# Three edits around the expert stage of a streaming-encoder block: skipped empty slots, a divided last load, one load issued earlier

## What is computed

```python
xf = x.reshape(B * T, D)                      # 512 x 1024
g_prob = softmax(xf @ rg_w + rg_b)            # 4 groups, the best one is taken
e_logits = ...                                # 8 experts in that group, top 2 taken, weights normalised
for g in range(N_GROUPS):                     # 4 groups x 8 experts = 32 experts
    hg = silu(xf @ w_gate[g]) * (xf @ w_up[g])        # 1024 -> 256
    y = y + (hg * combine[:, g]) @ w_down[g]          # 256 -> 1024
h = LayerNorm(alpha * h + y)
```

## Time and profile before

| | |
|---|---|
| median of 3 runs | 785.86 us (784.17 to 786.19) |
| the profiled execution | 784.38 us |
| its span | 782.6 us |
| granted TensorE clock, mean | 0.978 |
| TensorE matmul busy | 711.1 us, 91% |
| VectorE, ScalarE, GpSimd busy | 48%, 38%, 33% |
| DMA, mean over the span | 203 GB/s |
| weights of the experts | 96 MB in 96 loads of 1 MB |

### The profile page before, as it was taken

How to read it: one execution, slowest core, us unless ns; L and a number is a source line. 1 busy time by engine, 2 the same in 40 slices (tenths; PEclk the granted TensorE clock), 3 DMA queues, 4 the chain that set the end, 5 groups by cost and what they waited for, 6 DMA issues and landing times.

```text
span 782.6 us, 11844 instructions
## 1 busy us (share of the span) xinstructions
PE 711.1 (91%) x4296; PEld 501.9 (64%) x4296; DVE 377.2 (48%) x984; ACT 295.2 (38%) x604; POOL 259.9 (33%) x315
## 2 busy tenths in 40 slices
PE   7999999999999999999999999999999998887810
PEld 6865886777777777776888777655555554444400
DVE  2436998877577766648221346635211111111137
ACT  4345326667565555654320312123222222111111
POOL 3721541222234322137882000023333333233213
PEclk9999999999999999999999999999999999999965
DMA  8511231111123111016523690899999999999762
GB/s 229 160 54 55 60 102 54 55 55 54 55 61 102 55 55 54 30 33 226 173 80 108 233 384 28 304 397 417 416 417 419 418 417 419 417 417 418 326 226 121
DMA packets 57890, 158.57 MB, mean 203 GB/s; under 512 B 8558, under 2 KB 37238, under 8 KB 45552
## 3 DMA queue, kind: packets, MB, share of 16 engines
q1 hardware_dynamic: 52640, 149.15, 50.0%
q0 software_dynamic: 5200, 8.76, 3.1%
HBM read 153.60 MB, written 12.58 MB: 212 GB/s over the span
## 4 chain that ended last, share of the span: by engine, by line
PE 79%; DMA 9%; DVE 6%; SPq 2%; ACT 2%; issue 1%; POOL 0%; POOLq 0%; ACTq 0%; DVEq 0%
PE psum L849 36%; PE psum L1137 10%; DMA arena<-in_w_up_dram 7%; PE psum L1160 6%; PE psum L836 4%; PE psum L924 4%; PE psum L982 2%; PE psum L960 2%; PE psum L1056 2%; PE psum L830 2%; PE psum L976 2%; PE psum L782 1%; PE psum L894 1%; PE psum L1152 1%; DVE arena L1542 1%
## 5 line engine op out<-in xcount | busy, mean ns | idle before, releaser
L849 PE MATMUL psum<-arena,arena 128*128 128x512 f32 (+1 forms) x1296 | 316.9, 395 | 2.4 <-DVE arena L1542 1.3
L849 PEld LDWEIGHTS psum<-arena,arena 128*128 128x128 f32 x1296 | 235.1, 188 | 63.7 <-issue 15.4
L648 POOL TENSOR_TENSOR arena<-arena,arena 128x256 fp32r<-128x256 f32 (+1 forms) x139 | 145.1, 1079 | 237.5 <-ACT arena L1188 237.5
L1137 PE MATMUL psum<-arena,gate_a_T 128*64 128x256 f32 x1024 | 116.7, 380 | 11.5 <-DMA arena<-in_w_up_dram 11.4
L1137 PEld LDWEIGHTS psum<-arena,gate_a_T 128*64 128x64 f32 x1024 | 76.1, 137 | 60.7 <-issue 30.1
L1775 DVE COPY gate_a_T<-psum 128x128 f32<-128x128 f32 x32 | 9.4, 293 | 175.5 <-PE psum L1152 175.5
L1160 PE MATMUL psum<-arena,gate_a_T 128*64 128x512 f32 x256 | 62.0, 604 | 13.1 <-DVE gate_a_T L1775 13.1
L1188 ACT ACTIVATE arena<-arena 128x2048 fp32r<-128x2048 f32 x27 | 51.6, 1910 | 36.8 <-DMA arena<-in_w_branch_b_dram 26.7
L1278 ACT ACTIVATE arena<-arena,negm 128x193 f32<-128x193 f32 (+5 forms) x128 | 62.5, 493 | 3.6 <-DVE negm L1512 3.6
L1288 ACT ACTIVATE arena<-psum 128x1024 f32<-128x1024 f32 (+3 forms) x48 | 37.2, 775 | 69.5 <-PE psum L960 50.4
L728 POOL DMA_INDIRECT pair_rows<-gate_a_T,idx x32 | 33.2, 1038 | 62.3 <-ACT gate_a_T L1393 62.3
(11 more groups left out here) (233 smaller groups left out, 842.3 us busy)
## 6 DMA issues: line engine op xcount, KB each, us to landing
arena<-in_w_gate_dram SPq DMA_DIRECT2D x32, 1024.0 KB, 23.3
arena<-in_w_up_dram SPq DMA_DIRECT2D x32, 1024.0 KB, 27.2
arena<-in_w_down_dram SPq DMA_DIRECT2D x32, 1024.0 KB, 27.7
arena<-in_w_in_dram SPq DMA_DIRECT2D x19, 1024.0 KB, 5.3
arena<-in_w_branch_a_dram SPq DMA_DIRECT2D x4, 1024.0 KB, 5.2
arena<-in_w_branch_b_dram SPq DMA_DIRECT2D x4, 1024.0 KB, 5.3
arena<-in_w_out_dram SPq DMA_DIRECT2D x4, 1024.0 KB, 8.6
arena<-pair_rows SPq DMA_DIRECT2D x8, 512.0 KB, 7.3
```

The costliest lines, as they stand in the source:

```text
L648: nc.gpsimd.tensor_tensor(lo[:, k], raw[:, k], hi[:, k], ALU.subtract).then_inc(w_split, DT // n)
L849: ins = nc.tensor.matmul(ps[:, columns(kind)], wp[:, k, col:col + P], xp[:, k, columns(kind)], start=k == 0 and p == 0, stop=k == DT - 1 a ...
L1137: ins = nc.tensor.matmul(psum[CAP * g:CAP * g + CAP, 2 + s % 2, 0:FF], xgT[s % 2][:, k % 4, k // 4, :], ex_gu[slot][:, g, k, :], start=k = ...
```

## The change

Three edits that don't touch each other:

1. `tok_first` goes. The gathers of experts 2, 3 and 4 take their indices from `tok_i`, with the bounds check that the later gathers have, and wait for it.
2. Gate and up of expert 31 (slot 1, `LAST`) are loaded by four DMAs of 512 KB: k rows 0 to 3 of gate and of up, counted by a new semaphore `gu_front`, then k rows 4 to 7 of both. TensorE's `start(31)` waits for the front, and before k row 4 for the rest.
3. The load of down of expert 3 is issued right behind up of expert 4, ahead of the wait for `h1_ready` and the store of tile 3.

```diff
+LAST = (NE - 1) % EXS
...
-        tok_first = sb("tok_first", [P, XGS], I32)
...
+            def gate_up_part(e, slot, k0, k1, landed):
+                for g, w in enumerate((w_gate, w_up)):
+                    sp.dma_start(ex_gu[slot][:, g, k0:k1, :],
+                                 w[0, e].rearrange("(p k) f -> p k f", p=P)[:, k0:k1, :]).then_inc(landed, 16)
...
                     sp.wait_ge(unit_done, UNIT["out", 7] + 1)
                     up(4, 4)
+                    down(3, 3)
                 sp.wait_ge(h1_ready, t + 1)
                 sp.dma_start(h1_dram[2 * t * P:2 * (t + 1) * P, :].rearrange("(p h) c -> p (h c)", h=2), h1[:, t, :]
                              ).then_inc(h1_stored, 16)
-            down(3, 3)
             down(4, 4)
...
             for b in range((NE - EXS) // EXS * EXS, NE - EXS):
-                if b + 1 < NE - EXS:
+                if b + 2 < NE - EXS:
                     refill_gate_up(b + 1, b % EXS + 1)
+                elif b + 1 < NE - EXS:
+                    sp.wait_ge(gu_done, b + 2)
+                    gate_up_part(NE - 1, LAST, 0, DT // 2, gu_front)
+                    gate_up_part(NE - 1, LAST, DT // 2, DT, gu_landed[LAST])
                 refill_down(b, b % EXS)
...
                 pool.indirect_dma_start(out=xg[to], out_offset=None, in_=h1_dram,
-                                        in_offset=bass.IndirectOffsetOnAxis(ap=tok_first[:, n:n + 1], axis=0)
-                                        ).then_inc(xg_landed[to], 16)
-            pool.wait_ge(tok_ready, 2)
+                                        in_offset=bass.IndirectOffsetOnAxis(ap=tok_i[:, PEX + n:PEX + n + 1], axis=0),
+                                        bounds_check=2 * T - 1, oob_is_err=False).then_inc(xg_landed[to], 16)
...
-                pe.wait_ge(gu_landed[slot], use * 32 + 32)
+                if isinstance(b, int) and b == NE - 1:
+                    pe.wait_ge(gu_front, 32)
+                else:
+                    pe.wait_ge(gu_landed[slot], use * 32 + 32)
                 pe.wait_ge(xgt_copied, b + 1)
                 for k in range(DT):
+                    if isinstance(b, int) and b == NE - 1 and k == DT // 2:
+                        pe.wait_ge(gu_landed[slot], use * 32 + 32)
...
-            V.tensor_scalar(tok_first[:, :], psum[:, 7, PEX:AHEAD], dst_shift[:, 0:1], 0.0, ALU.add, ALU.max
-                            ).then_inc(tok_ready, 1)
```

More of the change, by code:

```diff
@@ L385, in build @@
         rows_done, rows_copied = sem("rows_done"), sem("rows_copied")
-        gu_landed = [sem(f"gu_landed{i}") for i in range(EXS)]
+        gu_landed, gu_front = [sem(f"gu_landed{i}") for i in range(EXS)], sem("gu_front")
         d_landed = [sem(f"d_landed{i}") for i in range(EXS)]
@@ L736, in _ @@
                 scatter(b, b)
-            pool.wait_ge(tok_ready, 3)
+            pool.wait_ge(tok_ready, 2)
             pool.wait_ge(dst_ready, 2)
@@ L1677, in _ @@
             weigh(TT - 1)
-            dve.wait_ge(tok_ready, 2)
+            dve.wait_ge(tok_ready, 1)
             pairs = oh.rearrange("p k t e -> p (k t) e")
@@ L1750, in over_tokens @@
                 tokens(psum[:, 7, 0:NTAB - NE], NE, NTAB - NE)
-                dve.wait_ge(tok_ready, 3)
+                dve.wait_ge(tok_ready, 2)
                 targets(psum[:, 7, 64:64 + NBLK - NE], NE, NBLK - NE)
```

## The result

The changed kernel takes 780.79 us (median of 13 runs, 777.91 to 783.52) against 785.04 us (13 runs, 782.71 to 786.24) for the kernel before, run beside it: a ratio of 0.9952, interval 0.9938 to 0.9967, or 3.8 us. Four comparisons of the same two kernels were made in all (the three others stand among the experiments): 0.9952, 0.9966, 0.9958 and 0.9945. Weighted by their intervals they give 0.9954 ± 0.0008, **3.6 us, 2.9 to 4.2**. The profiled execution took 779.60 us, its span 777.8 us.

The account below looks back on a forecast made before the run. The prediction took the last byte of weights to set the expert stage's end; down -1.1, empty slots -1.4 and split -0.6 summed to -3.1 us, taking the median from 785.86 to 782.8 us, range 781.3 to 785.8.

Parts of the forecast that it names:

- The bound: Expert stage: the last byte of weights sets the end; DMA time saved before it shortens the end while work is queued.
- Down of expert 3: Moved ahead of tile 3's store, its load fills the DMA gap at 502 to 506 us: -1.1 us, bounds 0 and -1.3.
- the first cover: First gather's start: tile 3's delayed store stays hidden behind the token table's last write, by 0.8 us at least.
- The second cover: After the first gather lands, another 2.1 us remain before TensorE turns its rows at 521.45.
- Empty slots: Three first gathers: 0.40 MB unmoved (0.95 us) and no slow row-0 reads (0.8 us); taken as -1.4 us, bounds 0 and -1.75.
- slow reads: 516 to 520 us: many gather slots reading one same row cut the rate to 335 GB/s, 0.8 us lost.
- The split: Last gate and up in two groups: TensorE's 0.62 us wait for the last up goes, -0.6 us.
- Rival 4: Last gate and up: each added DMA pays its fixed time, so slower by 1.2 us, 787.1 us; chance 0.06.
- The queue: Weights queue from 506 us on: stays fed, with about 1 us in hand each time, so savings count.
- Rival 2: Queue runs dry at 518 to 524 us and savings go idle: 0.9 us gained, 785.0 us; chance 0.12.
- Rival 1: Engines ending last gain little (gap 0.3, gathers 0.5, split 0.6): 1.4 us, 784.5 us; chance 0.2.
- The tail: Everything from the last scatter on was to be shifted as one.

Follow-up runs that it names:

- e1: Kernel before with only the three first gathers reading tok_i with a bounds check: 783.40 us, ratio 0.9981.
- e2: Kernel before with only the down of expert 3 issued ahead of tile 3's store: 783.59 us, ratio 0.9990.
- e7: The changed kernel, unedited, run a third time: 781.21 us, ratio 0.9958 to the kernel before.
- e6: Kernel before with each empty slot of the three first gathers fetching a row of its own instead of row 0: 783.46 us, ratio 0.9995.
- e10: Kernel before with all slots of the three first gathers out of bounds, rows of experts 2 to 4 unfetched: 782.46 us, ratio 0.9983.
- e3: Kernel before with only gate and up of the last expert cut in two groups: 784.09 us, ratio 0.9999.
- e13: Kernel before without the branch and code for overflowing experts on every engine: 783.81 us, ratio 0.9985.
- e12: Changed kernel without the branch and code for overflowing experts on every engine: 779.04 us, ratio 0.9941 to the kernel before.
- e14: The changed kernel, unedited, run once more to set the build without overflow code against: 780.31 us, ratio 0.9945.
- e8: Changed kernel with expert 30's gate and up also cut in two groups, last loop rounds written out: 781.30 us, ratio 0.9966.
- e9: Changed kernel less the split of the last gate and up (gathers and down together): 781.17 us, ratio 0.9967 to the kernel before.

## Why the prediction was right and where it was wrong

**The bound** held. In the expert stage less DMA work is an earlier end: what e1 and e2 save between 502 and 520 us is still there at expert 30, some 210 us later, as 1.7 and 0.8 us. How it gets there shows in TensorE's waits on line 1150 from 510 to 760 us, the view of the earlier trace rows:
```profile
  DMA arena<-in_w_up_dram: 8.6, 8
```
They were 12.9 us, 11 times, but one wait of 1.5 us stands twice in that row, once at the weight load and once at the matmul behind it: ten waits, 11.4 us. TensorE catches up with the weights one expert later: its waits began 174.6 us after tile 2's store, and now begin at 180.4 with one of 0.5 us. From 188.6 on they have the size they had (0.8 to 1.4 us each) and come 2.4 us earlier, as forecast, to the one before expert 30; and the last of them (0.62 us) is gone.

**Down of expert 3, forecast -1.1.** The steps were right up to the last: the gap is filled (0.72 to 0.99; idle 1.0 us to 0.04, though 0.2 us come back behind the store), down 3 issued at 498.08 (500.0 less the head start of 1.95), and the store, issued at 502.39, lands 6.4 us later at 508.8, or 510.8 in the time of the kernel before, half a microsecond past the forecast's 508.5 to 510.3. That was enough to undo the first cover. In the changed kernel tok_i is written at 508.54 and the store's last increment comes at 508.83; the gather, which needs both, starts 0.9 us behind the later of them, as it did before behind the table alone:
```profile
508.29 0.25 DVE L1678 SCALAR_TENSOR_TENSOR tok_i<-psum,dst_shift,strip 128x32 int32<-128x32 f32 x1
...
509.74 1.29 POOL L714 DMA_INDIRECT arena<-h_rows,tok_i  x1 [8.83 <-PE psum L1064]
```
Against tile 2's store it is 0.55 us later than in the earlier trace rows (21.92 against 21.37). The forecast's cover was measured from the wrong event: the gather stood 0.9 us behind tok_first, written at 510.25, and not 0.5 behind tok_i. So the wait for tok_i, put at nothing, costs 0.3 us (e1), and the store, which took up to 7.4 us, costs up to 1.0 more (22.7 in e7). The second cover took all that up: the rows landed by 517.8 (fifteen of the sixteen increments are in the trace), and TensorE turns them at 519.48, with 1.7 us of the 2.1 left. What failed is the size: a mean idle time was taken as the gain of the engine that ends last. It measured 0.8 us at expert 30 (0.8 timed, interval -0.3 to 1.9) in a profile whose store landed late; with an early landing the changed kernel's profiles are about 1 us further ahead.

**Empty slots, forecast -1.4.** Measured 1.5 us timed, 1.7 in the profile: the number stood, its working did not, and that is luck. The 0.8 us of slow reads are worth 0.2 at the end (e6). The bytes left out were 0.48 MB and not 0.40, since these three gathers hold fewer real rows than the mean gather: 1.15 us by the rate, not 0.95. They are worth about 1.5 at the end. That the engines that end last hold few real rows here, where I had argued that they hold more, would fit (e10) and is not shown.

**The split, forecast -0.6.** 0.9 us by the profile at the last matmul: the wait, and 0.22 us that the 32 records save when they follow other work without a pause, a term that the sum lacked. Timed alone it is 0.1 ± 1.3. Rival 4 fell: from 720 to 724 us, two fifths of the packets being those of the halves, the queue runs at 408 to 414 GB/s and a share of 1.00 to 1.04, and in e3 the last bytes landed when they had.

**The queue** stayed fed: 1.02 from 516 to 524. Rival 2, with its thin microsecond in hand, did not come about. Rival 1 was half right: its mechanism holds for the gap and for the slow reads, not for the bytes, where it had 0.5 us.

**The tail**, which was to be shifted as one, was not, in the profiles: 1.6 to 1.8 us of what is won by the last matmul are given back by the late increment. At the last matmul the four profiles of the changed kernel stand at 253.0 in the mean, the three of before (e13 among them) at 256.6: 3.6 us; at the pair load only 2.0 us are left. The timed difference is 3.6 us (2.9 to 4.2). One reading is that nothing is given back in executions without a profile. The other is that it is, and that the rest comes from elsewhere. The profiled executions themselves, all four of the changed kernel with the late increment, took 3.6 us less than the two of before (780.2 against 783.9 in the mean); besides the 2.0 us at the pair load, 1.1 us lie ahead of tile 2's store, where no edit reaches, and 0.5 us behind the pair load. Six profiles do not tell whether that 1.1 us is chance. e12, free of the late increment, was timed at 0.9941 beside 0.9945 for e14, where its profile is 2.8 us ahead at the pair load, 1.2 of it since before the last matmul. Set against each other, e12 and e13 have neither the packet nor the late increment, and their ratios are 3.5 us apart (± 1.8). Whether executions that are not profiled have the late increment stays open. The timings of e2, e8 and e9 fit better without it (e8 and e9, which have none, gained no more than their neighbours that do), that of e3 lies between the two, and no execution without a profile shows its increments.

**The number.** Two steps failed together. The gain was mis-sized, 3.1 us for 3.6 (3.8 in the comparison beside which it is read): +0.3 on the gathers, -0.4 on the down, +0.3 on the split (1.7 + 0.7 + 0.9 = 3.3 at the last matmul), and the parts together 0.3 us above their sum, 3.6 in the mean of four profiles. The three of these whose store landed late, as in e2, give 3.4, their sum; the fourth gives 4.4. The mis-sizing alone would have left the time in the range. The base was the other: 785.86, a median of three runs. The kernel before has since had medians of 785.04 (with those three among its 13), 784.52, 784.58, 784.03 and 784.92, each of 13 to 35 runs, 0.8 to 1.8 us lower. The low end gave all three upper bounds (3.7 us) but only 0.9 us of scatter, and 3.8 us of gain with a base lower by 0.8 us and the medians' own chance was past it. Of the 2.0 us between 782.8 and 780.79, the base makes 0.8, the gain 0.7 (3.8 for 3.1), and 0.5 is that the two medians lie 4.25 us apart where the ratio gives 3.8. The profiled execution at 784.38 had said that the base might be lower; the range should have started from there.

## What to carry to other kernels

In a stage that ends with the last byte, count DMA time for the engine that ends last, not for the mean of the sixteen: idle time and slow reads that the mean shows may be slack there (0.8 of 1.1 us, 0.2 of 0.9, each from one profile), while bytes left out were worth at least their mean (1.5 of 1.15 us). Where one transfer must be waited for at the end, let the first half of it be followed by work: two groups removed the wait at no cost in rate, and a second such cut gave nothing. A base of three runs was 0.8 to 1.8 us off here, against a gain of 3.6, and a profile of the changed kernel starts with its own chance (here 2 us by 26 us into the span), so compare distances from an event ahead of the edit, and take more than one profile: two of one kernel agreed to 0.15 us, four of another differed by 1.2.

## What the runs showed that was not expected

- Many reads of one row of DRAM cost rate: 332 to 335 GB/s at a full share, against 414 with the same bytes from different rows.
- A slot of a gather that is out of bounds keeps its packet (5200 in both) and moves no row.
- DMAs of half a MB in 4 KB pieces per partition, queued behind one another, pass at 408 to 414 GB/s, close to the 415 to 418 of those of 1 MB.
- A store of 0.5 MB behind a filled queue of loads landed after 4.0 to 4.4 us in four profiles and after 6.1 to 7.4 in five, and the weights behind it were about 1 us later in the second kind.
- 32 matmul records take 3.67 us after a wait and end 3.45 us behind the work ahead when there is none, at the same granted clock of 1.00.
- An instruction packet of 16 KB, 0.95 to 1.2 us long, holds the last few packets of the last scatter until its end in 9 of the 14 profiles that have it (last increment at 3.7 to 4.3 us instead of 2.3 to 2.4); in the two without it the scatter was short.
- The time to the 101st matmul record varied between 24.2 and 27.8 us over sixteen profiles of twelve builds, and between 24.2 and 26.3 over four of one build.
